# Softmax probabilities moved by sixteen small DMAs a tile, three tiles in four, and one load for the rows of the next branch

## The chip, the cores and the metric

The kernel runs on one core of one Trainium2 chip. The metric is the device time of one launch in microseconds. The profile is that of one execution; its rows give start times from the beginning of its span.

## The reference, cut to what matters

The layer has a token mixer (a gated linear attention, GLA, and a latent attention, MLA, then gates and a projection) and a mixture of 16 experts. The change lies in the latent attention, with 8 heads over 1024 tokens, and in the hand-over to the GLA branch that the kernel computes after it:

```python
def attend(qblk):                       # one block of 128 queries
    s = jnp.einsum('bhqd,bhkd->bhqk', qblk, k_t).astype(jnp.float32) * scale
    p = jax.nn.softmax(s, axis=-1)
    return jnp.einsum('bhqk,bhkd->bhqd', p.astype(v_t.dtype), v_t)
```

All values are float32. Each float32 product is made from three matmuls of high and low parts.

## The kernel before

**Tiles and steps.** The attention is written as a list of steps (i, n): head i (0 to 7), block n of 128 queries (0 to 7), and five steps more, (8, 0) to (8, 4), in which the last head is finished. Tile t = 8i + n is one block of probabilities, 128 queries by 1024 keys. Each of the engines runs its own program in order, and all of them walk over the same list of steps. Semaphores join them: `s_mm` (scores made), `max_ok` (row maximum made), `exp_ok` (exponentials made), `sq_ok` (tile block-transposed), `p_in` (transposed tile landed), `pt_hi` and `pt_lo` (its two parts made), `pv_mm` (half a head multiplied with the values), `ob_ev` (that half scaled into `obS`), `ob_out` (stored), `inv_out` and `inv_in` (inverse row sums stored and spread).

**One step on each engine.**

- TensorE: `scores(t)` (10 matmuls of 512 columns, waits for the exponentials of tile t-2), one `seam` (4 transposes for the next head's queries or keys), `probs_T(t-1)` if the tile before goes by TensorE (8 transposes), `values` (6 or 9 matmuls, at n = 0, 1, 2, 3, 4, 6, 7), `project` for later heads.
- VectorE (DVE): `probs_squares(t-1)` if that tile goes by DMA (one transposition of 32x32 blocks into the single buffer `squares_T`), `row_maximum(t)`, the low part of the seam, `probs_low(t-1)` for a tile from TensorE, `turned_low(t-3)` for a tile from DMA, and work for the next head.
- ScalarE (ACT): the high part of the seam, `probs_high(t-1)` or `turned_high(t-3)`, `exponentials(t)`, `take` of a projection. At (7, 6) and (8, 0) it also splits the first weights and rows of the GLA branch (`dense_hi`, `rows_high`).
- SyncE (SP) issues all DMAs of this stage, in order, and waits in between: `turn_probs(t-1)`, stores of inverse sums and of outputs, loads of the weights of later heads. A wait holds up everything behind it.

**Two ways for a tile.** The product with the values needs the probabilities with keys on partitions. By TensorE, a tile is transposed through PSUM. By DMA, DVE transposes its 32x32 blocks inside each quarter of the partitions, and DMAs carry each block row to its quarter. Before, every second tile (even t, up to 60) goes by DMA: four DMAs to DRAM, wait until they have landed, one DMA back.

**The next branch.** GLA needs the normalised rows again (`carry<-rows_T`, 8 pieces of 512 KB). `load_rows(k)` loads one piece and waits for the piece before it; two pieces are issued at each of the steps (7, 2), (7, 4), (7, 6), (8, 0).

## Time and profile before

| | us |
|---|---|
| time, median of 3 runs | 1960.42 (1959.71 to 1960.89) |
| the profiled execution | 1961.58 |
| its span | 1959.3 |
| TensorE busy in it | 1869.9 (95%) |
| DVE busy | 1373.2 (70%) |
| ACT busy | 1066.3 (54%) |
| mean granted TensorE clock | 0.983 |

The span is what the trace covers. TensorE is busy for all but 89 us of it. Register, semaphore and DMA-issuing instructions aren't counted as busy; DMA issues appear in the time line as SPq.

### The profile page before, as it was taken

Reading aid. Unit: us, or ns where it says so; the run is one execution under the profiler, and the core shown is the slowest. Engines: PE = TensorE matmul, PEld = TensorE weight load, DVE = VectorE, ACT = ScalarE, POOL = GpSimd, SP = SyncE. Lnnn points to the kernel's source line nnn. Section 1 sums busy time; section 2 is a strip of 40 time slices with the busy share of each in tenths; the row PEclk is TensorE's granted clock in tenths of the full one; section 3 lists DMA queues with packets and bytes.
Section 4 is the critical chain, followed back from the end, with each engine's and each line's share of the span. In section 5 each row is a group of like instructions: output and inputs, shape, how many; then the busy total and the mean of one; then the engine's idle time right before and its main releaser. Section 6 shows DMA issues by size and latency. Waiting matters only on the chain.

```text
span 1959.3 us, 26754 instructions
## 1 busy us (share of the span) xinstructions
PE 1869.9 (95%) x9179; PEld 1574.2 (80%) x9179; DVE 1373.2 (70%) x1829; ACT 1066.3 (54%) x1737; POOL 135.3 (7%) x147
## 2 busy tenths in 40 slices
PE   8989999999489999999999999997799999999997
PEld 8978888887368888888888888886688888888886
DVE  5477777777355657565765437835799898998986
ACT  6576666665244334242534222423677777877775
POOL 1021111010000000000000000000000101101010
PEclk9999999999789999999999999998899999999999
DMA  6125454554621111111454544343999999999993
GB/s 207 44 63 129 105 116 107 112 119 108 161 71 44 55 44 47 40 58 29 151 164 137 172 154 161 126 194 118 371 390 401 391 402 400 391 398 390 400 391 78
DMA packets 180666, 364.30 MB, mean 186 GB/s; under 512 B 29377, under 2 KB 99905, under 8 KB 180417
## 3 DMA queue, kind: packets, MB, share of 16 engines
q1 hardware_dynamic: 174784, 346.33, 51.6%
q0 software_dynamic: 4752, 16.78, 3.4%
q8 instruction: 55, 0.90, 0.2%
q14 instruction: 35, 0.28, 0.1%
q10 hardware_dynamic: 1040, 0.00, 0.0%
HBM read 308.37 MB, written 54.69 MB: 185 GB/s over the span
## 4 chain that ended last, share of the span: by engine, by line
PE 84%; DVE 6%; DMA 5%; ACT 2%; issue 1%; SPq 1%; POOL 1%; DVEq 0%; ACTq 0%; POOLq 0%
PE ps L1195 23%; PE ps L1197 23%; PE ps L1196 23%; PE ps L1184 5%; PE ps L1282 3%; PE ps L1491 1%; DMA probs_T<-squares_T 1%; PE ps L1503 1%; DMA carry<-rows_T 1%; PE ps L1321 1%; PE ps L1320 1%; DVE row_max L2042 1%; PE ps L1475 1%; PE ps L1501 1%; SPq L836 1%
## 5 line engine op out<-in xcount | busy, mean ns | idle before, releaser
L1807 DVE TENSOR_TENSOR w_lo<-w_raw,w_hi 128x1024 fp32r<-128x1024 f32 x384 | 442.6, 1218 | 54.8 <-ACT w_hi L3287 54.7
L3287 ACT ACTIVATE w_hi<-w_raw 128x1024 fp32r<-128x1024 f32 x384 | 371.0, 1053 | 0.5 <-PE ps L1197 0.4
L1195 PE MATMUL ps<-w_hi,xeT_hi 128*128 128x512 f32 x512 | 201.2, 393 | 1.0 <-DVE w_lo L1807 0.9
L1197 PE MATMUL ps<-w_hi,xeT_lo 128*128 128x512 f32 x512 | 199.8, 390 | 0.0
L1196 PE MATMUL ps<-w_lo,xeT_hi 128*128 128x512 f32 x512 | 199.2, 389 | 0.0
L1807 DVE TENSOR_TENSOR d_lo<-d_raw,d_hi 128x1024 fp32r<-128x1024 f32 (+1 forms) x66 | 67.2, 1027 | 143.2 <-ACT d_hi L2925 138.5
L1195 PE MATMUL ps<-hT_parts,d_hi 128*128 128x512 f32 x368 | 145.5, 395 | 0.0
L1197 PE MATMUL ps<-hT_parts,d_lo 128*128 128x512 f32 x368 | 144.1, 392 | 0.0
L1196 PE MATMUL ps<-hT_parts,d_hi 128*128 128x512 f32 x368 | 144.1, 392 | 0.0
L1102 POOL TENSOR_TENSOR stat<-stat,minus_half 128x4 f32<-128x4 f32 (+3 forms) x56 | 54.3, 970 | 1165.2 <-DVE stat L1804 1165.1
L2925 ACT ACTIVATE d_hi<-d_raw 128x1024 fp32r<-128x1024 f32 x42 | 44.5, 1060 | 157.1 <-PE ps L1197 87.7
L2042 DVE TENSOR_REDUCE row_max<-ps 128x1 f32<-128x1024 f32 x64 | 77.8, 1215 | 61.2 <-PE ps L1321 61.1
L1195 PEld LDWEIGHTS ps<-w_hi,xeT_hi 128*128 128x128 f32 x512 | 96.1, 188 | 21.3 <-DVE w_lo L1807 1.2
L1195 PE MATMUL ps<-d_hi,hT_parts 128*128 128x512 f32 x288 | 112.6, 391 | 0.0
L1197 PEld LDWEIGHTS ps<-w_hi,xeT_lo 128*128 128x128 f32 x512 | 96.1, 188 | 20.3
L1196 PE MATMUL ps<-d_lo,hT_parts 128*128 128x512 f32 x288 | 112.1, 389 | 0.0
L1197 PE MATMUL ps<-d_hi,hT_parts 128*128 128x512 f32 x288 | 112.1, 389 | 0.0
L1196 PEld LDWEIGHTS ps<-w_lo,xeT_hi 128*128 128x128 f32 x512 | 96.2, 188 | 19.5
L1195 PE MATMUL ps<-w_hi,act_T_hi 128*128 128x512 f32 x256 | 101.3, 396 | 0.8 <-ACT ye L3310 0.8
L1197 PE MATMUL ps<-w_hi,act_T_lo 128*128 128x512 f32 x256 | 99.9, 390 | 0.0
L1196 PE MATMUL ps<-w_lo,act_T_hi 128*128 128x512 f32 x256 | 99.6, 389 | 0.0
L1195 PEld LDWEIGHTS ps<-hT_parts,d_hi 128*128 128x128 f32 x368 | 69.8, 190 | 14.8 <-issue 0.4
(454 smaller groups left out, 4304.8 us busy)
## 6 DMA issues: line engine op xcount, KB each, us to landing
w_raw<-in_w_gate_e SPq DMA_DIRECT2D x128, 512.0 KB, 6.9
w_raw<-in_w_up_e SPq DMA_DIRECT2D x128, 512.0 KB, 7.0
w_raw<-in_w_down_e SPq DMA_DIRECT2D x128, 512.0 KB, 5.8
d_raw<-in_w_in SPq DMA_DIRECT2D x80, 256.0 KB, 3.3
probs_T<-squares_T SPq DMA_DIRECT2D x124, 128.0 KB
pT_lo<-probs_T SPq DMA_DIRECT2D x31, 512.0 KB, 3.4
gates_T<-stage SPq DMA_DIRECT2D x16, 512.0 KB, 2.9
sg<-gates_T SPq DMA_DIRECT2D x16, 512.0 KB, 3.5
```

Of the source, the lines that this page charges most:

```text
L836: sp.dma_start(rows[:, :, q, :], squares_T[q * SQ:(q + 1) * SQ].rearrange("b j c a -> b j (c a)")).then_inc(p_out, 16)
L1102: pool.tensor_tensor(dst, dst, minus_half[:, 0:dst.shape[1]], ALU.pow).then_inc(done, 1)
L1184: ins = pe.transpose(ps[0:rows, bank, j * P:(j + 1) * P], src, ident[:])
L1195: pe.matmul(out_ap, a_hi, b_hi, start=start, stop=False)
L1196: pe.matmul(out_ap, a_hi, b_lo, start=False, stop=False)
L1197: return pe.matmul(out_ap, a_lo, b_hi, start=False, stop=stop)
L1282: mm = pe.matmul(out_ap, src[:, k, toks], w[:, k, :], start=k == 0, stop=k == kc - 1)
L1320: pe.matmul(bank, qr_T[:, q], kr_T[i % 2][:, cols], start=False, stop=False)
L1807: return dve.tensor_tensor(dst, whole, high.bitcast(F32), ALU.subtract)
L2042: dve.tensor_reduce(row_max[:, n:n + 1], ps[:, 2 * (n % 2):2 * (n % 2) + 2, :], mybir.AxisListType.XY, ALU.max, negate=True).then_inc(max_ ...
L2925: nc.scalar.activation(d_hi[:, n % 2, :], d_raw[:, n % 2, :], ACT.Copy).then_inc(d_hi_ok, 1)
L3287: nc.scalar.activation(w_hi[:, n % RING, :], w_raw[:, n % RAW, :], ACT.Copy).then_inc(hi_ok, 1)
```

## The change

Three parts: (1) tiles 0 to 55 with t % 4 != 3 go by DMA (42 tiles instead of 31), none of the last head; each goes from `squares_T` straight to its place in SBUF by 16 DMAs of 32 partitions x 1 KB, without DRAM. The next block transposition waits until all 16 have landed. (2) The rows for GLA come in one DMA of 4 MB at step (7, 2). (3) `values` at n = 1 stands ahead of the scores of its step.

```diff
 def by_dma(t):
-    return 0 <= t < 8 * MH - 2 and t % 2 == 0
+    return 0 <= t < 8 * (MH - 1) and t % 4 != 3
...
             def turn_probs(t):
-                d, group = t // 2, t // Q4
-                sp.wait_ge(sq_ok, d + 1)
-                rows = p_dram[d % SLOTS].rearrange("(j b) q x -> b j q x", b=SQ)
-                for q in range(Q4):
-                    sp.dma_start(rows[:, :, q, :],
-                                 squares_T[q * SQ:(q + 1) * SQ].rearrange("b j c a -> b j (c a)")).then_inc(p_out, 16)
-                sp.wait_ge(p_out, 16 * Q4 * (d + 1))
-                if d:
-                    sp.wait_ge(p_in, 16 * d)
+                group = t // Q4
+                sp.wait_ge(sq_ok, dma_count(t))
                 if group >= 2:
                     sp.wait_ge(pv_mm, group - 1)
-                sp.dma_start(probs_part(pT_lo, t).bitcast(F32),
-                             p_dram[d % SLOTS].rearrange("p q (c a) -> p q c a", a=SQ)).then_inc(p_in, 16)
+                low = probs_part(pT_lo, t).bitcast(F32)
+                for q in range(Q4):
+                    for j in range(Q4):
+                        sp.dma_start(low[j * SQ:(j + 1) * SQ, q],
+                                     squares_T[q * SQ:(q + 1) * SQ, j]).then_inc(p_in, 16)
...
+                if m == 2 * MH - 1:
+                    sp.wait_ge(p_in, 16 * Q4 * Q4 * dma_count(NT * MH - 1))
...
+                    if i == MH - 1:
+                        sp.wait_ge(h_out, 32)
+                        sp.wait_ge(seam_tr, MH * 8)
+                        sp.dma_start(hT_again, h_dram.rearrange("k p s -> p k s")).then_inc(hT_in, 16)
...
-                if n % 2 == 0 and 8 * (MH - 1) + 2 <= 8 * i + n:
-                    for k in range(2):
-                        if 8 * i + n - 8 * (MH - 1) - 2 + k < KD:
-                            load_rows(8 * i + n - 8 * (MH - 1) - 2 + k)
...
             for i, n in STEPS:
+                if pv_at(i, n) and n == 1:
+                    values(*pv_at(i, n))
                 if i < MH:
                     scores(i, n)
...
-                if pv_at(i, n):
+                if pv_at(i, n) and n != 1:
                     values(*pv_at(i, n))
...
             def probs_squares(t):
                 dve.wait_ge(exp_ok, t + 1)
                 if t:
-                    dve.wait_ge(p_out, 16 * Q4 * (t // 2))
+                    dve.wait_ge(p_in, 16 * Q4 * Q4 * (dma_count(t) - 1))
```

DVE's order in head 2 shows the tiles that follow each other closely. Before, from the transposition of tile 20 to that of tile 22 (`row_max` is the row maximum of a step, `pT_lo<-pT_lo` is `turned_low`, `pT_lo<-ps` is `probs_low`):

```order
L2057 STREAM_TRANSPOSE squares_T<-probs 128x1024 [waits p_out,exp_ok]
L2042 TENSOR_REDUCE row_max<-ps 128x1 [waits s_mm]
L1807 TENSOR_TENSOR kr_lo<-ps,kr_T 128x512 [waits seam_hi]
L1807 TENSOR_TENSOR pT_lo<-pT_lo,pT_hi 128x1024 [waits pt_hi]
L2042 TENSOR_REDUCE row_max<-ps 128x1 [waits s_mm]
L2031 SCALAR_TENSOR_TENSOR qT_lo<-ps,qhn_c,qT_hi 128x512 [waits seam_hi]
L1807 TENSOR_TENSOR pT_lo<-ps,pT_hi 128x4x4x32 [waits pt_hi] x2
L1991 TENSOR_TENSOR qR<-qR,stat 128x4x192 [waits rstd]
L2057 STREAM_TRANSPOSE squares_T<-probs 128x1024 [waits p_out,exp_ok]
```

The same stretch of DVE's program now, tiles 20, 21 and 22:

```order
L2050 STREAM_TRANSPOSE squares_T<-probs 128x1024 [waits p_in,exp_ok]
L2035 TENSOR_REDUCE row_max<-ps 128x1 [waits s_mm]
L1800 TENSOR_TENSOR kr_lo<-ps,kr_T 128x512 [waits seam_hi]
L1800 TENSOR_TENSOR pT_lo<-pT_lo,pT_hi 128x1024 [waits pt_hi]
L2050 STREAM_TRANSPOSE squares_T<-probs 128x1024 [waits p_in,exp_ok]
L2035 TENSOR_REDUCE row_max<-ps 128x1 [waits s_mm]
L2024 SCALAR_TENSOR_TENSOR qT_lo<-ps,qhn_c,qT_hi 128x512 [waits seam_hi]
L1984 TENSOR_TENSOR qR<-qR,stat 128x4x192 [waits rstd]
L2050 STREAM_TRANSPOSE squares_T<-probs 128x1024 [waits p_in,exp_ok]
```

A third transposition stands between the two, one step after the first, and each waits for `p_in` of the one before; the row maximum of the step is behind it.

SP's order in the last head, before (from the store of head 6's first half, step (7, 2)):

```order
L829 DMA mla_out_T<-obS 128x512 [waits ob_ev]
L859 DMA obS<-inverse_sums 128x512 [waits ob_out,inv_out]
L867 DMA carry<-rows_T 128x1024 [waits seam_tr,h_out]
L867 DMA carry<-rows_T 128x1024 [waits hT_in]
L836 DMA probs_T<-squares_T 32x4x256 [waits sq_ok]
L836 DMA probs_T<-squares_T 32x4x256 x3
L843 DMA pT_lo<-probs_T 128x1024 [waits pv_mm,p_in,p_out]
L851 DMA inverse_sums<-row_inv 128x4x1 [waits inv_in,inv_ok]
L829 DMA mla_out_T<-obS 128x512 [waits ob_ev]
L867 DMA carry<-rows_T 128x1024 [waits hT_in] x2
```

and now, from the same store up to the first weights of GLA (`d_raw`) at step (7, 6):

```order
L830 DMA mla_out_T<-obS 128x512 [waits ob_ev]
L858 DMA obS<-inverse_sums 128x512 [waits ob_out,inv_out]
L879 DMA carry<-rows_T 128x8x1024 [waits seam_tr,h_out]
L848 DMA inverse_sums<-row_inv 128x4x1 [waits inv_in,inv_ok]
L830 DMA mla_out_T<-obS 128x512 [waits ob_ev]
L858 DMA obS<-inverse_sums 128x512 [waits ob_out,inv_out]
L778 DMA d_raw<-in_w_in 128x4x128 x4
```

The waits for each piece of the rows and for the tiles of the last head are gone from SP's queue.

## Rows read from the trace of the kernel before

**Rows 1.** The page's busy time: engine, us, share, instructions.
```profile
PE 1869.9 (95%) x9179; PEld 1574.2 (80%) x9179; DVE 1373.2 (70%) x1829; ACT 1066.3 (54%) x1737; POOL 135.3 (7%) x147
```

**Rows 2.** Windows of head 2 and of the end of attention.
```profile
core 0: us, PE busy (x) PEld busy (x) DVE busy (x) ACT busy (x) POOL busy (x), PEclk, DMA share, GB/s
...
224.10:275.60 51.50, 51.13 (x289) 43.96 (x289) 39.34 (x60) 31.98 (x79) 5.53 (x5) 1.00 0.51 114
...
481.00:568.20 87.20, 52.90 (x226) 42.69 (x225) 37.87 (x42) 29.79 (x41) 3.19 (x6) 0.84 0.55 130
```

**Rows 3.** SP's turn issues to DRAM of tile 0, tile 8, tile 56, and its last.
```profile
131.35 1.81 SPq L836 DMA_DIRECT2D probs_T<-squares_T  x4
...
172.58 2.38 SPq L836 DMA_DIRECT2D probs_T<-squares_T  x4
...
481.06 1.77 SPq L836 DMA_DIRECT2D probs_T<-squares_T  x4
...
520.34 1.89 SPq L836 DMA_DIRECT2D probs_T<-squares_T  x4
```

**Rows 4.** Block transpositions (31), minimum, median, maximum ns, first and last start.
```profile
L2057 DVE STREAM_TRANSPOSE squares_T<-probs x31: 1211/1239/1247, 130.1 to 507.0; 128x1024 f32<-128x1024 f32 x31
```

**Rows 5.** SP's time line in head 2: start, us, line, transfer, count.
```profile
234.59 0.43 SPq L829 DMA_DIRECT2D mla_out_T<-obS  x1
238.70 0.32 SPq L859 DMA_DIRECT2D obS<-inverse_sums  x1
```

**Rows 6.** SP's time line at 683 us, small DMAs in a row.
```profile
683.47 1.27 SPq L805 DMA_DIRECT2D w_a<-in_gla_wa_f  x3
684.83 1.29 SPq L805 DMA_DIRECT2D w_a<-in_gla_wa_b  x3
686.22 0.37 SPq L807 DMA_DIRECT2D b_a<-in_gla_ba_f  x1
```

**Rows 7.** Time from issue to landing of line 805's DMAs (8 KB each).
```profile
DMA to landing us min/median/max: 1.5/2.0/3.0
```

**Rows 8.** Windows between the transpositions of tiles 18 and 20, and 22 and 24.
```profile
236.73:253.08 16.35, 16.35 (x93) 14.38 (x92) 11.92 (x24) 9.71 (x26) 2.01 (x2) 1.00 0.46 142
262.74:274.33 11.59, 11.41 (x66) 9.60 (x65) 9.31 (x19) 7.55 (x19) 0.00 (x0) 1.00 0.48 158
```

**Rows 9.** TensorE's time line in the last head and after, idle time before in brackets.
```profile
484.30 1.03 PE L1184 MATMUL ps<-ident,probs 128*128 128x128 f32 x8
485.09 0.48 PE L1195 MATMUL ps<-pT_hi,v_hi_even 128*128 128x512 f32 x1
...
498.30 1.82 PE L1184 MATMUL ps<-ident,probs 128*128 128x128 f32 x8 [4.10 <-ACT probs L2916]
...
538.59 1.97 PE L1184 MATMUL ps<-ident,probs 128*128 128x128 f32 x8 [17.44 <-ACT probs L2916]
...
568.19 1.19 PE L1403 MATMUL ps<-gateT,w_a_split 80*128 80x512 f32 x2 [7.04 <-DVE w_a_split L1807]
```

**Rows 10.** SP's time line in the last head.
```profile
526.29 2.08 SPq L777 DMA_DIRECT2D d_raw<-in_w_in  x4
528.41 7.58 SPq L867 DMA_DIRECT2D carry<-rows_T  x2
```

**Rows 11.** ACT's time line in the last head.
```profile
532.65 1.06 ACT L2925 ACTIVATE d_hi<-d_raw 128x1024 fp32r<-128x1024 f32 x1 [16.25 <-DMA d_raw<-in_w_in]
```

**Rows 12.** The page's DMA issues: count, KB each, median us to landing.
```profile
d_raw<-in_w_in SPq DMA_DIRECT2D x80, 256.0 KB, 3.3
...
carry<-rows_T SPq DMA_DIRECT2D x12, 512.0 KB, 4.4
```

**Rows 13.** The page's bytes moved, GB/s in 40 slices.
```profile
GB/s 207 44 63 129 105 116 107 112 119 108 161 71 44 55 44 47 40 58 29 151 164 137 172 154 161 126 194 118 371 390 401 391 402 400 391 398 390 400 391 78
```

**Rows 14.** DVE's outputs of head 6's first and head 7's second half.
```profile
484.16 0.69 DVE L2078 TENSOR_TENSOR obS<-ps,obS 128x512 f32<-128x512 f32 x1
...
561.40 0.69 DVE L2078 TENSOR_TENSOR obS<-ps,squares_T 128x512 f32<-128x512 f32 x1 [11.03 <-DMA mla_out_T<-obS]
```

More of the change, by code:

```diff
@@ L64 @@
 Q4 = P // SQ
-SLOTS = 4
 LATE = NT - 2
@@ L168, in tensor_count, with dma_count @@
     return sum(by_tensor(u) for u in range(t + 1))
+def dma_count(t):
+    return sum(by_dma(u) for u in range(t + 1))
 def parts_count(t):
@@ L236, in hybrid_layer @@
     h_dram = nc.dram_tensor("rows_T", (KD, P, S), F32, kind="Internal").ap()
-    p_dram = nc.dram_tensor("probs_T", (SLOTS, P, Q4, NT * SQ), F32, kind="Internal").ap()
     inv_dram = nc.dram_tensor("inverse_sums", (2, HALF), F32, kind="Internal").ap()
@@ L541, in hybrid_layer @@
         sq_ok = sem("sq_ok")
-        p_out = sem("p_out")
         p_in = sem("p_in")
@@ L639, in hybrid_layer @@
         s_sig = Later(latT_act, 7)
-        g_out = [Later(h_out, 32), Later(hT_in, 16 * KD)]
+        g_out = [Later(h_out, 32), Later(hT_in, 16)]
         rows_out = Later(inv_out, 32 * MH)
@@ L858, in spread_inverse @@
                     sp.wait_ge(ob_out, 16 * m)
+                if m == 2 * MH - 1:
+                    sp.wait_ge(p_in, 16 * Q4 * Q4 * dma_count(NT * MH - 1))
                 sp.dma_start(inverse_at(h, half), spread(inv_dram[half], HALF)).then_inc(inv_in, 16)
-            def load_rows(k):
-                if k == 0:
-                    sp.wait_ge(h_out, 32)
-                    sp.wait_ge(seam_tr, MH * 8)
-                else:
-                    sp.wait_ge(hT_in, 16 * k)
-                sp.dma_start(hT_again[:, k, :], h_dram[k]).then_inc(hT_in, 16)
             load_ukv(2)
@@ L2903, in turned_high @@
             def turned_high(t):
-                act.wait_ge(p_in, 16 * (t // 2) + 16)
+                act.wait_ge(p_in, 16 * Q4 * Q4 * dma_count(t))
                 nc.scalar.activation(probs_part(pT_hi, t), probs_part(pT_lo, t).bitcast(F32), ACT.Copy).then_inc(pt_hi, 1)
@@ L2910, in exponentials @@
                 if by_dma(t - 2):
-                    act.wait_ge(sq_ok, (t - 2) // 2 + 1)
+                    act.wait_ge(sq_ok, dma_count(t - 2))
                 elif t >= 2:
@@ L2957, in rows_high @@
             def rows_high(k):
-                act.wait_ge(hT_in, 16 * (k + 1))
+                act.wait_ge(hT_in, 16)
                 nc.scalar.activation(hT_hi[:, k, :], hT_again[:, k, :], ACT.Copy,
```

## The prediction, as it was made

> **What bounds the kernel now.** I read the page's busy times first: TensorE is busy for 95% of the span [rows 1]. Then I cut the attention into windows of one head each, since a mean over 1959 us says nothing about this stage [rows 2]. The reader is to see that head 2 (heads 1 and 3 to 5 read alike) takes 51.5 us with TensorE busy for 51.1 of them and DVE for 39.3: TensorE sets the pace there, about 6.4 us a step. From SP's turn of tile 0 at 131.35 to that of tile 8 at 172.58, head 0 takes 41.2 us; from tile 0 to tile 56, at 481.06, the seven heads take 349.7 us [rows 3]. The last window is another matter: 87.2 us with only 52.9 us of TensorE, and its granted clock is 0.84 where the others have 1.00 [rows 2]. The time line of that window shows gaps in front of TensorE, of 4.10, 17.44 and 7.04 us, and one more between the first two [rows 9]. So two stretches are to be judged: seven heads in which TensorE must not be starved, and an end in which it is.
>
> **One tile by sixteen DMAs.** In the changed order each transposition of a DMA tile waits for `p_in` of the DMA tile before, and the row maximum of the step stands behind that transposition in DVE's queue. Tiles 0, 1, 2 of every four stand in steps that follow each other, so one cycle is: transpose, issue 16, land, transpose again.
>
> - The transposition: 1.24 us [rows 4].
> - Issues: SP's smallest DMAs in a row, 16 rows of 512 bytes, start 0.46 us apart: from 683.47 to 686.22 there are six intervals, 2.75/6 = 0.458 [rows 6]. The present turns, each DMA four times larger than a new one, take 1.77 us for four, 0.44 each, when nothing holds them up [rows 3]. Size makes no difference in these rows, so I take 0.46 for a DMA of 32 KB: the sixteenth starts 15 x 0.46 = 6.9 us after the first.
> - Landing: 1.5/2.0/3.0 us for DMAs of 8 KB from DRAM into SBUF [rows 7]. The trace has no transfer from SBUF to SBUF, so this is the nearest row; I take 1.7, between its least and its median, since the new ones leave DRAM out, and keep 1.5 and 2.7 for the bounds.
> - Sum of a cycle: 1.24 + 6.9 + 1.7 = 9.8, with about 0.1 for two hand-overs by semaphore 9.9 us, against steps of 6.4.
>
> TensorE can't hide it: `scores(t)` wait for the exponentials of t-2, these for the row maximum, and that is behind the transposition. ACT is held up in the same way.
>
> **A head, interval by interval.** Tiles 0 to 1, 1 to 2, 4 to 5, 5 to 6 are direct cycles: 4 x 9.9 = 39.6. From 2 to 4 there are two steps, and DVE's own work counts: between the transpositions of tiles 18 and 20 it is busy for 11.92 us [rows 8]; one more `turned_low` (1.2) and waits of some 0.4 make 13.5. In step (i, 2) SP stores `obS`, and the load after it comes 4.1 us later [rows 5]; SP is then about 2.0 us late for tile 2, a cycle of 11.9, which the 13.5 cover. From 6 to the next head's 0 DVE has 9.31 [rows 8] + 1.2 = 10.5. Together 63.6 us for heads 1 to 5. Head 0 has five cycles and one of 10.4, since no head before it is finished there: 59.9. Head 6 has no next but one to prepare: 4 x 9.9 + 11.9 + 10 = 61.5. Sum: 59.9 + 5 x 63.6 + 61.5 = 439.4, against 349.7: **+90 us**.
> What TensorE saves in these heads (28 tiles by transposes before, 14 after, 0.79 us each, 484.30 to 485.09 in [rows 9]; 11 us) is worth nothing while it waits for the chain. Nor does a lower clock after each gap cost, as steps of 9.9 us have room for 6.4 us of work partly at half speed. SP alone would fit: 48 x 0.46 = 22 us for every four steps and some 2 besides, in 25.8; it is the single buffer that puts transposition, issue and landing in a row.
>
> **`values` at n = 1 ahead of the scores.** Six matmuls move ahead of ten in TensorE's queue, so a half of the head is ready about 2.3 us earlier, `turn_probs` of the next group no longer waits for `pv_mm`, and the scores come 1.4 us later. All of it lies inside steps that the chain holds up: 0. If the chain didn't, it would lie beside a busy TensorE, and be 0 again.
>
> **The end of attention.** The three tiles of head 7 that went by DMA now cost 3 x 0.79 = 2.4 us of TensorE and take away the turns that SP stood in. The first two gaps go: both waited for exponentials [rows 9], which stood in ACT's queue behind a turned tile. So does part of the third: ACT waited 16.25 us for `d_raw` [rows 11], whose load SP issued only at 526.29, between pieces of the rows of which each waits for the one before [rows 10].
> When does it go on now? I keep the clock of before for the start of head 7. The last seam is long done; the 4 MB follow the store of the half that DVE finished at 484.85 [rows 14] by the 4.1 us of [rows 5] and an issue: 489.5. At 390 GB/s, as in the experts [rows 13], they take 10.7 us, and 1.5 to start: 501.7. The stores of step (7, 4) go through the same queue, so they land at about 502.5; then SP spreads the inverse sums and issues the first weights, done at 504; they land 3.3 us later [rows 12]. ACT splits weights and a row (2 x 1.06 [rows 11]), takes tile 62's high parts and the last exponentials (1.1 + 1.3): 513 with the hand-overs. So the transposes that started at 538.59 [rows 9] start at 513: **25 us** earlier. TensorE's own work would be done at about 506, so a gap of some 7 us stays.
> The fourth gap: DVE waited 11.03 us for the first half's store [rows 14], which SP issued behind the last two pieces, and then had the low parts of four rows to make ahead of the gate weights. Now the rows are there and SP is free; TensorE's 22.6 us of work between its last two gaps (568.19 - 7.04 - 538.59) leave time for all but 1.5 us. 5.5 us of gap go, and about 1.5 us by a clock that falls less far (eight transposes took 1.97 us behind the long gap, 1.03 without one [rows 9]): **7 us**. The end together: **-32 us**.
>
> **Sum.** +90 - 32 = +58 us on the profiled execution's 1961.58 (span 1959.3, the rest lies around it): 2019.6. It stands 1.2 us above the median of the runs: 2018.
>
> **Two rules against each other.** The trace puts 0.46 us on each issue [rows 6]. The Trainium skill, DMA: Bandwidth & Descriptors, section SWDGE vs HWDGE vs iDMA, says that the sequencer's time to start a DMA is usually small beside the DMA itself; by that the cycle would be little more than transposition and landing, and the time that of the first rival. The same page's Rules for kernel authors says to coalesce, since transfers under 64 KB pay mostly overhead. The trace is with the second: its small DMAs cost SP as much as large ones.
>
> **The rivals.**
>
> - *The chain fits behind TensorE (faster).* The place is the transposition's wait for `p_in`, the price the cycle. Were sixteen issues overlapped, so that a cycle takes under 6.4 us, nothing would be lost in the heads, 11 us of transposes saved and 32 us gained at the end: 1961.6 - 43 = 1919, 1917 by the median. On the way there the loss falls by 30 us for each us of cycle (30 of the 42 intervals are bound by it), so gain and loss meet at 8.0 us, that is at 0.33 us an issue with the same landing. For it: an issue by itself takes 0.32 us [rows 5]. Against it: in a row they come 0.44 to 0.46 apart for every size in the trace.
> - *Issues stall as they do now (slower still).* SP's turn issues of before, from the group at 131.35 to the one at 520.34, 31 groups of four [rows 3], sum up to 68.3 us, 0.55 each. With that mean the cycle is 11.2 us and more intervals are bound by it: 30 x 1.3 + 5 x 0.7 = 42 us more, 2060. With a landing of 2.7 on top it would be near 2100.
> - *The end gives little back.* The 4 MB stand ahead of the stores and of the first weights in the same queue. If they run at the 4.4 us of a 512 KB piece by itself [rows 12], 35 us in all, ACT waits to about 536 and the end gives 9 us: 2041.
> - *Gain and loss cancel*, at a cycle of about 8.0 us: 1960.
>
> **Chances.** The forecast, with a cycle between 9.1 us (0.42 an issue, landing 1.5: 24 us less) and 10.7 (25 us more): 0.60, its own range 1994 to 2043. Stalls 0.13, little back 0.13, chain fits or nearly 0.12, cancel 0.02. To hold 8 in 10 I go down to a cycle of 8.4 us (0.37 an issue, the shortest of [rows 6] with the pause behind it taken as nothing, and 1.5) and up past the stalls: 1972 to 2066. A measurement of this kernel tells changes over about 0.2%, 4 us, from none. Faster by more: 0.12; within: 0.02; slower: 0.86.
>
> **What would show it.** In the profile after: transpositions of tiles 0, 1, 2 of a group start 9.9 us apart, each after several us of DVE idle until a DMA landed; SP's sixteen issues of a tile take 7.3 us; heads 1 to 5 take about 63 us with TensorE busy for 50 or so of them; the chain that ended last has SP's issues and DMAs in it through the seven heads. In the last head one gap of about 7 us stands ahead of the last tile's transposes. It is wrong if sixteen issues take under 5.5 us, if DVE doesn't wait for `p_in`, or if the gap at the weights stays near 17 us.

## The result, and the profile after

The changed kernel takes 2180.6 us (2179.0 to 2183.9), the kernel before 1960.3 beside it: a ratio of 1.113, 95% interval 1.111 to 1.1145. Slower was right; +58 us was forecast and it is +220, far outside the range of 1972 to 2066 us.

The page of the changed kernel: busy times, the clock that TensorE was granted in 40 slices, and the chain that ended last, by engine and by line.

```profile
PE 1918.5 (88%) x9091; PEld 1609.6 (74%) x9091; DVE 1384.3 (64%) x1829; ACT 1069.3 (49%) x1726; POOL 135.8 (6%) x147
...
PEclk9988888987987899999999999999979999999999
...
PE 70%; SPq 14%; DVE 7%; DMA 4%; ACT 2%; issue 2%; POOL 1%; DVEq 0%; ACTq 0%; POOLq 0%
PE ps L1186 20%; PE ps L1188 20%; PE ps L1187 20%; SPq L840 13%; PE ps L1175 3%; DMA pT_lo<-squares_T 3%; DVE squares_T L2050 2%; PE ps L1273 2%; PE ps L1484 1%; PE ps L1496 1%; DMA mla_out_T<-obS 1%; DVE row_max L2035 1%; PE ps L1468 1%; P
```

SyncE's issues of line 840, the sixteen small DMAs, are 13% of the chain. TensorE has fewer instructions than before [rows 1] and is busy for 49 us more: it is stretched by its clock, not by work. Head 1, from the transposition of tile 8 to that of tile 16, as a window (columns as in [rows 2]: length, busy time of PE, PE's loads, DVE, ACT and POOL, granted clock, DMA share, GB/s):

```profile
208.90:294.60 85.70, 57.51 (x274) 48.79 (x273) 41.27 (x62) 32.45 (x77) 5.55 (x4) 0.84 0.23 56
```

85.7 us where head 1, like the head 2 of [rows 2], took 51.5, at a granted clock of 0.84 where it was 1.00. Heads 1 to 5 take 82.2 to 87.7 us (forecast about 63), with TensorE busy for 56 to 58 of them. The group of `squares_T`, with its duration in ns (least, median, most), its waits, and the time to landing:

```profile
L840 SPq DMA_DIRECT2D pT_lo<-squares_T x672: 507/591/5441, 131.3 to 713.4; - x168
L2050 DVE STREAM_TRANSPOSE squares_T<-probs x42: 1233/1245/1247, 130.0 to 702.7; 128x1024 f32<-128x1024 f32 x42
...
  DMA pT_lo<-squares_T: 241.7, 29
...
DMA to landing us min/median/max: 1.8/1.8/8.1
```

So DVE stood 241.7 us, 29 times, in front of a transposition. [Rows 4] showed 31 transpositions in 377 us; now there are 42 in 573. SyncE's and DVE's time lines from the last tile of head 0 on and in head 1:

```profile
195.96 10.01 SPq L840 DMA_DIRECT2D pT_lo<-squares_T  x16
208.79 0.37 SPq L848 DMA_DIRECT2D inverse_sums<-row_inv  x1
210.51 25.60 SPq L840 DMA_DIRECT2D pT_lo<-squares_T  x32
236.15 0.58 SPq L830 DMA_DIRECT2D mla_out_T<-obS  x1
```

```profile
224.83 1.25 DVE L2050 STREAM_TRANSPOSE squares_T<-probs 128x1024 f32<-128x1024 f32 x1 [7.00 <-DMA pT_lo<-squares_T]
237.44 1.25 DVE L2050 STREAM_TRANSPOSE squares_T<-probs 128x1024 f32<-128x1024 f32 x1 [8.93 <-DMA pT_lo<-squares_T]
```

Sixteen issues take 10.0 us (forecast 7.3), 0.633 us from start to start, and two transpositions in a row start 12.6 us apart: 1.24 + 15 x 0.633 + 1.8, and 0.1 for the hand-overs. The end of attention (the answer to [rows 9 to 11]), on TensorE's, ACT's and SyncE's time lines:

```profile
762.03 1.97 PE L1175 MATMUL ps<-ident,probs 128*128 128x128 f32 x8 [14.48 <-ACT probs L2909]
...
786.62 0.78 PE L1396 MATMUL ps<-gateT,w_a_split 80*128 80x512 f32 x2 [1.91 <-DVE w_a_split L1800]
```

```profile
756.09 1.06 ACT L2918 ACTIVATE d_hi<-d_raw 128x1024 fp32r<-128x1024 f32 x1 [12.78 <-DMA d_raw<-in_w_in]
```

```profile
728.54 0.38 SPq L879 DMA_DIRECT2D carry<-rows_T  x1
735.47 0.37 SPq L848 DMA_DIRECT2D inverse_sums<-row_inv  x1
736.05 0.34 SPq L830 DMA_DIRECT2D mla_out_T<-obS  x1
749.93 0.33 SPq L858 DMA_DIRECT2D obS<-inverse_sums  x1
750.32 2.08 SPq L778 DMA_DIRECT2D d_raw<-in_w_in  x4
```

The gap at the gate weights is 1.9 us where it was 7.0, but the one ahead of the last tile is still 14.5: ACT waits for weights that SyncE can't issue until the stores of the inverse sums and of the output's half, issued at 735.47 and 736.05, have landed, 14 us later. I had the 4 MB of line 879 in mind for that wait. The experiments will put it elsewhere.

### The profile page after: what moved, and what is told of

The parts are those of the page before. It is cut to its first block, busy times and chain, and to the rows that moved or that the text cites. A ratio compares the mean times of both kernels' runs of the same rounds, so it can differ in the third digit from the quotient of the medians.

```text
span 2177.1 us, 27084 instructions
## 1 busy us (share of the span) xinstructions
PE 1918.5 (88%) x9091; PEld 1609.6 (74%) x9091; DVE 1384.3 (64%) x1829; ACT 1069.3 (49%) x1726; POOL 135.8 (6%) x147
## 4 chain that ended last, share of the span: by engine, by line
PE 70%; SPq 14%; DVE 7%; DMA 4%; ACT 2%; issue 2%; POOL 1%; DVEq 0%; ACTq 0%; POOLq 0%
PE ps L1186 20%; PE ps L1188 20%; PE ps L1187 20%; SPq L840 13%; PE ps L1175 3%; DMA pT_lo<-squares_T 3%; DVE squares_T L2050 2%; PE ps L1273 2%; PE ps L1484 1%; PE ps L1496 1%; DMA mla_out_T<-obS 1%; DVE row_max L2035 1%; PE ps L1468 1%; PE ps L1494 1%; DVE affT L2668 1%
## 5 line engine op out<-in xcount | busy, mean ns | idle before, releaser
L2050 DVE STREAM_TRANSPOSE squares_T<-probs 128x1024 f32<-128x1024 f32 x42 | 52.2, 1243 | 242.0 <-DMA pT_lo<-squares_T 241.7
L2909 ACT ACTIVATE probs<-ps,row_max 128x1024 f32<-128x1024 f32 x64 | 71.5, 1117 | 192.2 <-DVE row_max L2035 192.2
L1273 PE MATMUL ps<-w_uq_h,cqT 128*128 128x192 f32 x384 | 84.1, 379 | 64.8 <-DVE d_hi L2024 28.8
L1273 PEld LDWEIGHTS ps<-w_uq_h,cqT 128*128 128x128 f32 x384 | 75.9, 224 | 72.6 <-DVE d_hi L2024 31.5
L1186 PE MATMUL ps<-w_kv_hi,ckvT_hi 128*128 128x256 f32 x96 | 36.3, 378 | 97.7 <-DVE qT_lo L2024 67.5
```

The costliest lines, as they stand in the source:

```text
L1186: pe.matmul(out_ap, a_hi, b_hi, start=start, stop=False)
L1273: mm = pe.matmul(out_ap, src[:, k, toks], w[:, k, :], start=k == 0, stop=k == kc - 1)
L2050: dve.transpose(squares_T[:], probs[:, t % 2, :].rearrange("p (c j b) -> p j c b", c=NT, j=Q4)) \
L2909: nc.scalar.activation(probs[:, t % 2, :].rearrange("p (a c) -> p a c", a=2), ps[:, 2 * (n % 2):2 * (n % 2) + 2, :], ACT.Exp, bias=row_max ...
```

## Experiments

Medians, each beside runs of the kernel before on the same chip (1960.3 to 1965.5 us there); ratios are to those. e2, e8, e9 and e13 leave out a part of the computation, which the text of each names; m1 to m3 are small kernels with one execution each.

```
kernel                                             us      ratio (95% interval)
changed kernel                                     2180.6  1.113  (1.111 - 1.1145)
e1  every second tile within SBUF                  1993.9  1.0165 (1.0148 - 1.0182)
e2  four DMAs a tile                               2005.7  1.0221 (1.0204 - 1.0238)
e3  two halves, two semaphores                     2117.4  1.0789 (1.0771 - 1.0807)
e4  two queues                                     2095.0  1.0680 (1.0662 - 1.0698)
e5  before + rows in one load, values, last head   1953.2  0.9942 (0.9929 - 0.9956)
e6  e5 with the rows in two loads                  1951.8  0.9936 (0.9922 - 0.9949)
e7  before + values moved                          1973.2  1.0045 (1.0031 - 1.0059)
e8  changed kernel, sums in 128 pieces             2154.8  1.0986 (1.0967 - 1.1004)
e9  e2, sums in 128 pieces                         1958.2  0.9982 (0.9972 - 0.9991)
e10 e6, sums block-transposed before the store     1936.4  0.9868 (0.9851 - 0.9884)
e11 e10, values moved in the last head alone       1927.5  0.9834 (0.9820 - 0.9847)
e12 before, sums block-transposed                  1937.2  0.9882 (0.9866 - 0.9897)
e13 e4, sums in 128 pieces                         2056.5  1.0485 (1.0469 - 1.0501)
```

My theory after the result: the chain that I had described, with an issue of 0.63 us in place of 0.46. Its rivals: that copies within SBUF get in each other's way or in the engines', that the clock is the cause and not the consequence, that something else holds the transposition.

### What one issue costs

m1, issues alone. Two of its ten series as code:

```
for q in range(Q4):                                       # within SBUF, series 1
    for j in range(Q4):
        sp.dma_start(low[j*SQ:(j+1)*SQ, q, 0:256], sq[q*SQ:(q+1)*SQ, j]).then_inc(done, 16)
for q in range(Q4):                                       # to DRAM, series 2
    for j in range(Q4):
        sp.dma_start(dr_b[q, j*SQ:(j+1)*SQ, 0:256], sq[q*SQ:(q+1)*SQ, j]).then_inc(done, 16)
```

> A kernel that leaves the layer out: SyncE alone issues series of 16 DMAs, each series ended by a wait for all of them and run four times, in this order: (1) the changed kernel's 16 copies within SBUF, 32 partitions x 1 KB each; (2) the same from SBUF to DRAM; (3) the same from DRAM to SBUF; (4) within SBUF, 128 partitions x 1 KB; (5) within SBUF, 16 partitions x 1 KB; (6) within SBUF, 32 x 4 KB; (7) SBUF to DRAM in the form of the kernel before, 32 x 4 x 1 KB; (8) within SBUF, 1 partition x 1 KB; (9) four DMAs of 32 x 4 KB within SBUF; (10) one DMA of 128 x 4 KB. Theory (an issue costs by its kind: both sides in SBUF 0.63 us, one in DRAM 0.46): series 1, 4, 5, 6 and 8 all near 0.63, series 2, 3 and 7 near 0.46. Rival (the cost goes by the number of descriptors): 1 partition and 16 partitions cheaper than 32, 128 partitions dearer. Rival (the cost comes from the queue filling up with DMAs that are not yet done): the first issues of a series at 0.46 and the later ones slower, and 128 x 1 KB slower than 32 x 1 KB. Landing after the last issue 1.5 to 2 us in each.

The groups of its lines 270 to 303, series 1 to 8 in the order of that text (duration of the issue in ns, least, median, most; first and last start):

```profile
L270 SPq DMA_DIRECT2D low<-sq x64: 507/591/592, 47.0 to 90.5; - x64
...
L275 SPq DMA_DIRECT2D dr_b<-sq x64: 302/421/423, 92.4 to 124.5; - x64
...
L280 SPq DMA_DIRECT2D low<-dr_a x64: 302/421/438, 126.1 to 159.2; - x64
...
L284 SPq DMA_DIRECT2D low<-sq x64: 465/601/603, 161.1 to 205.4; - x64
...
L289 SPq DMA_DIRECT2D low<-sq x64: 507/589/591, 207.5 to 250.8; - x64
...
L294 SPq DMA_DIRECT2D low<-sq x64: 507/591/598, 252.5 to 297.2; - x64
...
L298 SPq DMA_DIRECT2D dr_b<-sq x64: 302/446/466, 299.5 to 340.4; - x64
...
L303 SPq DMA_DIRECT2D low<-sq x64: 497/589/591, 344.5 to 387.1; - x64
```

Read the medians against the names on the left: every group from SBUF to SBUF has 0.59 to 0.60 us, whether 1, 16, 32 or 128 partitions and whether 1 KB or 128 KB; every group with one side in DRAM has 0.42 to 0.45. The distance from start to start is 0.04 more, 0.63 and 0.46 (0.64 for 128 partitions in series 4, 0.49 for the 128 KB of series 7). The least duration in a group (0.507 and 0.302) is that of an issue after a wait, not in a row. Landing after the last issue was 1.8 us in series 1. The price hangs on where the two sides lie, and on nothing else that I varied by more than 0.03 us. A second such kernel (m2, series 5 and 6) added that a copy within the same partitions and one from DRAM to DRAM also cost 0.59: both sides in the same kind of memory. Theory confirmed; the rivals of piece count and of a filling queue fell.

### How many issues, through what

e2, four issues a tile:

```diff
                 for q in range(Q4):
-                    for j in range(Q4):
-                        sp.dma_start(low[j * SQ:(j + 1) * SQ, q],
-                                     squares_T[q * SQ:(q + 1) * SQ, j]).then_inc(p_in, 16)
+                    j = (q + 1) % Q4
+                    sp.dma_start(low[j * SQ:(j + 1) * SQ], squares_T[q * SQ:(q + 1) * SQ]).then_inc(p_in, 16)
```

> The changed kernel with 4 DMAs a tile in place of 16: each takes a quarter of the transposed tile (32 partitions x 4 KB) to the next quarter's partitions, so that the same 512 KB move within SBUF for the same 42 tiles, but the blocks are not sorted to their places (that part of the computation is left out). Theory (the number of issues is what costs): cycle 1.24 + 4 x 0.63 + 1.8 = 5.6 us, under a step of 6.4, the wait at the transposition goes, heads near 52 us, 1935 to 1965 us. Rival (bytes within SBUF or their landing cost): the wait stays, over 2100 us.

With the same bytes in a quarter of the issues 175 of the 220 us go: it is their number that costs, not bytes within SBUF. (The pieces are also fewer and larger here, 4 KB in place of 1 KB; that an issue's price doesn't go by them is m1's result.) Transpositions in a row start 5.5 us apart, as expected (5.6). But 2005.7 is above my 1965: DVE still waited 74.8 us. One wait shows where, on SyncE's and on DVE's time line:

```profile
210.22 0.37 SPq L847 DMA_DIRECT2D inverse_sums<-row_inv  x1
212.41 0.34 SPq L830 DMA_DIRECT2D mla_out_T<-obS  x1
213.56 10.48 SPq L840 DMA_DIRECT2D pT_lo<-squares_T  x5
```

```profile
222.26 1.25 DVE L2049 STREAM_TRANSPOSE squares_T<-probs 128x1024 f32<-128x1024 f32 x1 [5.89 <-DMA pT_lo<-squares_T]
```

Four issues from 213.56 are out by 216.0 (the fifth of the row belongs to the next tile), yet the transposition that waits for them starts at 222.26: over 6 us to land in place of 2.7, its median here. In the transfers' records of this run eleven stretches up to 520 us show packets of 1 to 3 us each (4 KB take 0.3 otherwise), and each begins 4 to 7 us after a store of inverse sums. In the kernel before, 15 such stretches of 4 to 8 us follow 15 stores by 3 to 7 us. That store, `inverse_sums<-row_inv`, writes 512 pieces of 4 bytes. e8 and e9 below test it.

e1, fewer tiles:

```diff
 def by_dma(t):
-    return 0 <= t < 8 * (MH - 1) and t % 4 != 3
+    return 0 <= t < 8 * (MH - 1) and t % 2 == 0
```

> The changed kernel with every second tile of heads 0 to 6 turned within SBUF (28 tiles, 16 DMAs each) in place of three of four; the last head by TensorE, rows of the next branch in one load, as in the changed kernel. Theory (16 issues at 0.63 us in a chain with the transposition and the landing, 12.6 us a tile): the chain fits under two steps of the kernel before (2 x 6.4 = 12.9 us), so the transposition's wait on the DMAs all but goes; heads near 53 us, and the time is that of before less what the end gives (10 to 15 us) plus a few microseconds where an issue stalls: 1950 to 1975 us. Rival (copies from SBUF to SBUF slow the engines or the other transfers, whatever the chain): 28/42 of the growth stays, 2100 us or more, without waits at the transposition. Rival (the growth is in TensorE's clock): heads over 56 us, 2000 us.

1993.9: most of the growth goes, but I had expected 1950 to 1975, and DVE still waited 55.0 us, 17 times, for the copies. "Two steps are 12.9 us" was a mean again. In the kernel before the intervals between the transpositions of a head are 9.3, 12, 13.9 and 16.3 us; the chain lifts the first two to 12.6, and the long ones, full of TensorE's work, don't shrink for it. That is 4 us a head; heads 3 and 4 take 62 us each (53 to 57 the others), and copies are held up there as in e2: sixteen issues from 325.65 on, 3.6 us behind a store of inverse sums, take 15.5 us in place of 10.0. The rival of 28/42 of the growth (2100) fell. The rival of the clock had named 2000 us, close to this; but head 1, 55 us long, had a granted clock of 1.00, so that it grew without it. In heads 3 and 4, at 0.94 and 0.95, TensorE was busy for 1.4 and 3.2 us longer than before, of 10 to 11 us that they grew by.

e3, without the single buffer's chain:

```diff
-                dve.transpose(squares_T[:], probs[:, t % 2, :].rearrange("p (c j b) -> p j c b", c=NT, j=Q4)) \
-                    .then_inc(sq_ok, 1)
+                for j in range(2):
+                    if t:
+                        dve.wait_ge(p_in[j], 32 * Q4 * (dma_count(t) - 1))
+                    dve.transpose(squares_T[:, 2 * j:2 * j + 2],
+                                  probs[:, t % 2, :].rearrange("p (c j b) -> p j c b", c=NT, j=Q4)[:, 2 * j:2 * j + 2]) \
+                        .then_inc(sq_ok, 1)
```

> The changed kernel with the tile transposed in two halves, each with its own semaphore: the first half of the next tile is transposed once the first 8 DMAs of this one have landed, while the last 8 are issued. The 16 DMAs a tile stay. Theory (the wait is a chain of issue, landing and transposition through one buffer; without the last two SyncE's issue alone bounds it): a tile costs 16 x 0.633 = 10.1 us in place of 12.6, with SyncE's other work and its stalls 64 to 70 us a head in place of 82: 2065 to 2100 us. Rival (what holds the transposition is not the buffer but, for instance, the time at which the exponentials are ready): no change, 2170 to 2190 us.

2117.4, above my 2065 to 2100. The heads fell from 85 to 76.5 us, so that the chain through the one buffer was part of it, against the rival; sixteen issues (10.0 us a tile) remain. My 64 to 70 a head left out the stretches after the stores, which this trace has too (a transposition at 324.12 waits 9.0 us for copies issued behind the store at 311.02). What they cost here no run separates; in the changed kernel it is 3 us a head (e8), so that they needn't be all of what I missed.

e4, the issues shared; SyncE keeps `q` 0 and 1, and ScalarE has this ahead of the exponentials:

```diff
+            def turn_probs(t):
...
+                act.wait_ge(sq_ok, dma_count(t))
...
+                for q in range(2, Q4):
+                    for j in range(Q4):
+                        nc.scalar.dma_start(low[j * SQ:(j + 1) * SQ, q],
+                                            squares_T[q * SQ:(q + 1) * SQ, j]).then_inc(p_in, 16)
...
+                if i < MH and by_dma(8 * i + n - 1):
+                    turn_probs(8 * i + n - 1)
                 if i < MH:
                     exponentials(i, n)
```

> The changed kernel with 8 of a tile's 16 DMAs issued by ScalarE's queue (ahead of the exponentials of the next tile) and 8 by SyncE's. Theory (serial issue on one engine): 1.24 + 8 x 0.63 + 1.8 = 8.1 us a tile, per four tiles 2 x 8.1 and 12.9 = 29 us, heads 58 us, if ScalarE's issues cost it no more than SyncE's: 2010 to 2040 us; ScalarE, which waited 192 us for DVE, takes 8 x 0.63 us a tile in that time. Rival (the DMA engines or SBUF serve these copies one after the other, and the issue only shows it): the pitch of each queue doubles to 1.2 us, and the time stays at 2180 us or grows.

2095.0 where I had expected 2010 to 2040, heads of 73 us. ScalarE's time line:

```profile
245.15 5.31 ACTq L2908 DMA_DIRECT2D pT_lo<-squares_T  x8
250.56 1.11 ACT L2920 ACTIVATE probs<-ps,row_max 128x1024 f32<-128x1024 f32 x1 [5.58 <-issue]
```

Eight issues take 5.3 us there while SyncE issues its eight, so the pitch doesn't double and the DMA engines aren't what is served in turn. But ScalarE computes nothing meanwhile: the exponentials come 5.6 us later. I had given it that time, and it is on the path (DVE waited 59.1 us for exponentials, and still 81.3 us for copies). The Trainium skill, DMA: Bandwidth & Descriptors, section Issuing engines are not separate DMA queues, says that issuing on several engines only saves the sequencer's time, "usually small relative to the DMA itself". The first half agrees with this run. The second doesn't: 0.6 us for each DMA against 1.8 us to landing, and eight of them hold the engine 5.3 us.

### The end of attention

e7, one part alone:

```diff
             for i, n in STEPS:
+                if pv_at(i, n) and n == 1:
+                    values(*pv_at(i, n))
                 if i < MH:
                     scores(i, n)
```

> The kernel before with the product with the values ahead of the scores at the second step of each head, and nothing else. I forecast 0 for this. Theory: the same time within 0.2% (1956 to 1964 us). Rival: the row maximum of the second tile comes later by the product's length in each head and TensorE waits for the exponentials, 8 x 1 to 3 us slower, 1968 to 1985 us.

1973.2, 0.45% or 9 us slower than before in place of 0. Up to 480 us TensorE's waits at line 1282 (queries' projection, for DVE's `qr_T`) are 9.6 us in six times, and 1.1 us before: 1.4 us in each head. The later scores delay the row maximum, and behind it DVE's low part of the query. My "beside a busy TensorE" overlooked that TensorE next reads what DVE makes behind that maximum. What it costs in the changed kernel, where the chain holds those steps, no run shows.

e5, the change's end without its heads (with the change's edits to the rows and to `values` in the kernel before), and e6, e5 with the rows in two loads:

```diff
-    return 0 <= t < 8 * MH - 2 and t % 2 == 0
+    return 0 <= t < 8 * (MH - 1) and t % 2 == 0
```

```diff
-                        sp.dma_start(hT_again, h_dram.rearrange("k p s -> p k s")).then_inc(hT_in, 16)
+                        sp.dma_start(hT_again[:, 0:2], h_dram[0:2].rearrange("k p s -> p k s")).then_inc(hT_in, 16)
...
                     load_gla(0, 1)
+                    sp.dma_start(hT_again[:, 2:], h_dram[2:].rearrange("k p s -> p k s")).then_inc(hT_in, 16)
```

> The kernel before, with its turning through DRAM, and only the parts of the change at the end: the last head all by TensorE, the product with the values ahead of the scores at the second step, the rows of the next branch in one load of 4 MB. My forecast of this part was -32 us; the changed kernel's trace shows -10 us up to the last tile's transposition and -15 us up to the gate logits. Theory (the part is worth what the trace shows): 1945 to 1950 us. Rival (the gain was made only because the changed kernel's heads left room ahead of it): 1960 us or more.

> As the run before it, but the 4 MB of rows in two loads: the first two blocks (1 MB) where the one load stood, the other six (3 MB) behind the loads of the next branch's weights. Theory (the small store of the inverse sums and the weights wait behind the 4 MB in the DMA queues, which holds the exponentials' engine 12.8 us before the last tile): the wait of 12.8 us goes to a few, another 8 to 12 us gained, 1935 to 1942 us. Rival (the weights are not late for the rows' sake, or the rows are then late themselves at the step that reads the third block): no more than 2 us either way.

e5 has 1953.2, between my 1945 to 1950 and the rival's 1960: 0.58% under its runs of before, 11 us, with e7's loss in it. The end's other parts are worth some 20 us, so the gain isn't lent by the changed kernel's heads. e6 has 1951.8 where I had expected 1935 to 1942, no difference from e5 that can be told. TensorE's last gap in e6, and SyncE ahead of it:

```profile
534.89 1.97 PE L1177 MATMUL ps<-ident,probs 128*128 128x128 f32 x8 [11.85 <-ACT probs L2911]
```

```profile
502.19 1.01 SPq L880 DMA_DIRECT2D carry<-rows_T  x1
510.97 0.37 SPq L851 DMA_DIRECT2D inverse_sums<-row_inv  x1
511.55 0.34 SPq L829 DMA_DIRECT2D mla_out_T<-obS  x1
522.89 0.33 SPq L859 DMA_DIRECT2D obS<-inverse_sums  x1
```

Only 1 MB of rows is ahead now and the spreading load still goes out 12 us after the store of the sums. My theory for e6, that the 4 MB hold it, fell: the gap was 13.35 us in e5, so that 3 MB less ahead took 1.5 us off it. The store's own 512 pieces were left.

### The store of the inverse sums

e8 and e9, in the changed kernel and in e2:

```diff
-                sp.dma_start(inv_dram[half].rearrange("(t p) -> p t", p=P), row_inv[:, Q4 * half:Q4 * half + Q4],
-                             allow_slow_non_contiguous=True).then_inc(inv_out, 16)
+                sp.dma_start(inv_dram[half].rearrange("(p t) -> p t", p=P),
+                             row_inv[:, Q4 * half:Q4 * half + Q4]).then_inc(inv_out, 16)
```

> The changed kernel with the inverse sums stored in 128 pieces of 16 bytes in place of 512 of 4 bytes (so they are not put in the order of the rows: that part of the computation is left out). Theory (each of these stores is followed by a stretch of about 6 us in which copies take 2 to 3 us each; where it falls on a tile's 16 copies the chain waits): two stores a head, some hit an idle moment of the queue; the changed kernel's trace shows two landings or issues held by 5 us and some smaller: 10 to 50 us less than 2180, 2130 to 2170 us. Rival (the stretches don't come from this store): 2175 to 2185 us. The chain of 12.6 us a tile stays in both, so the time stays over 2100 us.

> The kernel with four DMAs a tile (blocks not sorted) and the inverse sums in 128 pieces of 16 bytes (not in the order of the rows). With four DMAs the time was 2005.7 us, heads of 60 us, and the one long wait a head (6 to 8 us) lay on copies issued 3 to 5 us after the store of inverse sums. Theory: that wait goes, heads 53 to 54 us, 1950 to 1970 us. Rival (the long wait has another cause): 2000 to 2010 us.

2154.8 and 1958.2, both as the theory had it: 26 and 48 us for one store's form. The stretches of slow packets are gone: by the count that gives the 15 in the kernel before (five or more packets of up to 4 KB and over 1 us each, close together), neither trace has one. In head 2 of e8 the transpositions stand 13.3, 12.6, 16.9, 12.9, 12.7 and 13.7 us apart, and the end reads:

```profile
738.18 1.97 PE L1175 MATMUL ps<-ident,probs 128*128 128x128 f32 x8 [6.03 <-ACT probs L2909]
```

```profile
720.07 0.32 SPq L848 DMA_DIRECT2D inverse_sums<-row_inv  x1
720.65 0.32 SPq L830 DMA_DIRECT2D mla_out_T<-obS  x1
726.09 0.32 SPq L858 DMA_DIRECT2D obS<-inverse_sums  x1
```

The 4 MB load is still one piece, and the gap is 6.0 us in place of 14.5; I had forecast 7. The last spreading load waits for the store of sums alone: it follows that by 1.4 us (741.62 to 743.03), and by 8.2 us in the changed kernel (765.47 to 773.62). So the forecast of the end was missed by what it didn't look at.

e12, with the whole computation kept and in the kernel before; e10 and e11 put it beside e6's end:

```diff
-                dve.reciprocal(row_inv[:, at], row_sum[:, at]).then_inc(inv_ok, 1)
+                dve.reciprocal(row_inv[:, 0:Q4], row_sum[:, at]).then_inc(inv_ok, 1)
+                dve.wait_ge(inv_ok, 2 * m + 2)
+                dve.transpose(inv_T[:], row_inv[:]).then_inc(inv_ok, 1)
...
+                for q in range(Q4):
+                    sp.dma_start(inv_dram[half].rearrange("(t q b) -> q t b", q=Q4, b=SQ)[q],
+                                 inv_T[q * SQ:q * SQ + Q4]).then_inc(inv_out, 16)
```

> The kernel before, with nothing changed but the store of inverse sums: block-transposed in SBUF and stored by 4 DMAs of 4 pieces of 128 bytes (all of the computation kept). Theory (the stretches of slow packets after the stores cost the kernel before as well): with it the 12 us of waits at the transposition and some of the end go, 1944 to 1952 us; together with the end's parts it gave 15 us. Rival (it paid only beside the changed end): 1956 to 1962 us.

> The kernel with turning through DRAM, the end as in the changed kernel and the rows in two loads (1951.8 us), and the inverse sums block-transposed in SBUF ahead of their store, which then is 4 DMAs of 4 pieces of 128 bytes in place of one of 512 pieces of 4 bytes (all of the computation is kept). Theory (the stretches of slow packets that follow the stores go): in the kernel before they lie mostly under TensorE's work; the waits that they make are 12 us in all, half of it on the path: 1940 to 1950 us, a few us less than the run without. Rival (all of it is hidden, and the 3 issues and two small operations more cost): 1951 to 1956 us.

> The kernel with turning through DRAM, the rows in two loads and the inverse sums block-transposed before their store (1936.4 us), with the product with the values ahead of the scores in the last head alone, where the all-TensorE turning needs it, in place of every head. Theory (in the heads before it the move makes TensorE wait 1.6 us a head for DVE's low part of the query's rotary rows, which gave 9 us alone): 7 to 10 us less, 1926 to 1931 us. Rival (with the other changes that wait is hidden): 1934 to 1938 us.

e12 takes 1937.2, 23 us less than before and more than I had expected (8 to 16); e10 takes 1936.4, also below my 1940. In e12 the first six heads are as long as before (tile 48 is transposed at 429.3 us, 429.9 before), though DVE's waits for copies at the transposition, 12.3 us before, go down to 0.9; some 3 us are made in head 6 (tile 56 at 476.5, 479.8 before) and the rest at the end. TensorE's gaps there, 14.9 us in all, to hold against 34.3 before, the 4.10, 17.44 and 7.04 of [rows 9] and this one:

```profile
512.70 1.97 PE L1184 MATMUL ps<-ident,probs 128*128 128x128 f32 x8 [5.71 <-ACT probs L2916]
```

```profile
501.41 1.97 PE L1186 MATMUL ps<-ident,probs 128*128 128x128 f32 x8 [2.78 <-ACT probs L2923]
...
520.32 1.97 PE L1186 MATMUL ps<-ident,probs 128*128 128x128 f32 x8 [10.20 <-ACT probs L2923]
...
545.14 0.70 PE L1405 MATMUL ps<-gateT,w_a_split 80*128 80x512 f32 x2 [1.91 <-DVE w_a_split L1809]
```

e11, with `values` moved in the last head alone (tile 56's high parts would otherwise overwrite what the last product of head 6's first half reads), takes 1927.5:

```diff
-                if pv_at(i, n) and n == 1:
+                if pv_at(i, n) and (i, n) == (MH - 1, 1):
                     values(*pv_at(i, n))
```

That is 9 us less than e10, as e7 said, and 1.7% less than before. Against e12 it is 10 us less: with the short store the other parts of the end are worth half of their 20 us in e5. Its gap ahead of the last tile:

```profile
513.50 1.97 PE L1179 MATMUL ps<-ident,probs 128*128 128x128 f32 x8 [3.58 <-ACT probs L2918]
```

e13, e4 with e8's edit:

> The kernel with a tile's 16 DMAs issued 8 by SyncE and 8 by ScalarE (2095.0 us), and the inverse sums in 128 pieces of 16 bytes (not in the order of the rows). Theory (what it has over the 2010 to 2040 us that I worked out is in part the slow stretches after the stores, in part ScalarE's issues, which hold the exponentials): 25 to 50 us of it go, 2045 to 2070 us. Rival (it is ScalarE's issues alone): 2085 to 2097 us.

2056.5, heads of 68 us, 38 us under e4: the stores have their part in e4's excess, as the theory had it. DVE's wait of 59.1 us for ScalarE stays, which fits ScalarE's issues as the other part; no run takes them out alone.

m2 and m3, the store by itself, first with a wait behind it, then without:

```
sp.dma_start(inv_d[0:512].rearrange("(t p) -> p t", p=P), sq[:, 0, 0:4], allow_slow_non_contiguous=True)
sp.dma_start(inv_d[512:1024].rearrange("(p t) -> p t", p=P), sq[:, 0, 0:4])
```

> A kernel that leaves the layer out: SyncE alone issues, four times each, (1) 32 copies within SBUF of 32 partitions x 1 KB; (2) the store of inverse sums as the kernels have it (512 elements of 4 bytes, each a piece of its own, to DRAM), a wait for it, and the 32 copies; (3) the same with the store in 128 pieces of 16 bytes; (4) the spreading load of the sums from DRAM to 128 partitions, a wait, and the 32 copies; (5) 16 copies of 32 x 1 KB whose source and target are the same partitions; (6) 16 copies of 32 x 1 KB from DRAM to DRAM. Theory (in the layer, packets of other transfers take 2 to 3 us each in a stretch of about 6 us that begins 3 to 5 us after each store of inverse sums, because of its 512 pieces): series 2 alone shows packets over 1 us or a landing or an issue of 3 us and more; in 3 there are none or shorter ones. Rival (the stretch comes from something else in the layer, such as instruction fetches of the busy engines): none in any series. The issue: 0.63 us in 1, 5 and 6 (both sides in the same memory) by the first series of measurements; a rival that only crossing between partitions costs has 5 at 0.46.

> A kernel that leaves the layer out: SyncE issues, four times each, (1) three sets of 16 copies within SBUF (32 partitions x 1 KB), a wait after each set; (2) the store of 512 pieces of 4 bytes and, with no wait for it, the same three sets; (3) the store of 128 pieces of 16 bytes and the same. In the measurement before, a wait for the first store took 8 to 9 us and for the other 1.1 us, and copies after the wait ran as ever. Theory (the store holds the DMA engines for those 8 us): in series 2 the first set of 16 is done 3 to 8 us late or an issue in it takes 3 us and more, in 3 nothing does. Rival (the store's pieces wait in the memory alone and copies pass them): the sets of series 2 take as long as those of series 1, and the layer's slow stretches need the layer's other traffic.

SyncE's time line in m2: the store of 512 pieces (line 278), then that of 128 (line 283), each with the copies that wait for it:

```profile
132.64 0.40 SPq L278 DMA_DIRECT2D inv_d<-sq  x1
140.98 20.14 SPq L272 DMA_DIRECT2D low<-sq  x32
...
253.47 0.34 SPq L283 DMA_DIRECT2D inv_d<-sq  x1
254.89 20.13 SPq L272 DMA_DIRECT2D low<-sq  x32
```

8.3 us against 1.4 for 2 KB either way; landings of 8.0 to 9.3 us in all four. The copies behind the wait run as ever (20.1 us for 32). In m3 the copies don't wait, and of four sets of 48 behind the large store one took 34.7 us and one 33.3, the others 32.5 and 32.6 like those without it. So I expected too much of m3: by itself the store is slow to complete but lets copies pass with 0 to 2 us of delay. Why copies in the layer are held for 5 us is open; that they are, and no longer are with the store's other form, e9 shows. The Trainium skill, DMA: Bandwidth & Descriptors, section Rules for kernel authors, says that a last dimension that isn't contiguous becomes a descriptor for each element and should be rearranged. This trace agrees: the window of one store has 528 packets in the first form and 144 in the second, and the rearranged one lands after 1.4 us in place of 8.3.

## Why the prediction was wrong

- **The mechanism stood.** The single buffer puts transposition, issue and landing in a row; DVE waits for `p_in`, the row maximum and the exponentials stand behind it. The transposition (1.24) and the landing (1.7 forecast, 1.8) were right.
- **The term that failed is the issue**, "0.46 for a DMA of 32 KB". It is 0.633 when both sides are in SBUF. My rows were from DRAM to SBUF and from SBUF to DRAM [rows 3, 6]; they showed that size makes no difference, and I concluded that kind doesn't either. The cycle is 12.6 in place of 9.9. 28 direct intervals at 2.7 us are 76 us. In e8 those 28 take 13.0 us in the mean, so +87; the 11 us more lie in intervals where SyncE has other DMAs to issue between.
- **The two-step intervals**, 13.5 and 10.5 us by DVE's own work, were measured at 16.7 and 13.7 (e8, means over heads 1 to 5): +43 in the seven heads. Two steps failed. TensorE's window in [rows 8] was 16.35 us and full, and I summed DVE's 11.92. And "Nor does a lower clock after each gap cost" is wrong there (in e8's interval from tile 10 to tile 12, 17.0 us, TensorE is busy for 14.0 at a granted clock of 0.80 and waits 3.0): the projection of line 1273, 2.2 us for twelve matmuls at full clock, takes 3.6 and 3.8 us behind the waits at 227.9 and 240.5, at a granted clock of 0.84 over the head. How much of the 43 us is the clock's and how much the full window's is not shown.
- **The stretches after the stores** weren't in the sum: 14 us in the heads and 10 us at the end (changed kernel against e8).
- **The end**, -32 forecast: with the stores' stretches gone it lacks 6 us up to the last tile (49.4 us from tile 54's transposition, forecast 43.4) and no more behind it. The step that failed is "they land at about 502.5", 0.8 us behind the 4 MB: the stores took 14 us, and 5.4 with the sums in 128 pieces (e8). The rival "the end gives little back" blamed the 4 MB; e6 says that this was the wrong suspect, though the 9 us that it gave the end back are near the changed kernel's 10 up to the last tile.
- **`values`, 0:** wrong in its second half ("0 again" if the chain didn't hold): 9 us (e7). For the changed kernel itself no run tests the 0 alone.
- Together 87 + 43 + 14 + 10 + 6 = 160 of the 162 us that were missed. These are differences between the forecast and the traces, stretch by stretch, so that they must come near the whole; the causes of the 87, 14 and 10 have experiments behind them, those of the 43 and the 6 only the traces.
- **The rival of stalls** was priced at 0.55 an issue from [rows 3]. The true cost was above even that, so no case of mine held it. No row showed the operation at all; a price for it that is multiplied by 15 and then by 42 asked for a bound of its own above the rows, and the range had only the stalls' 0.55.

## What to carry to other kernels

Price an issue by its kind (which memories the two sides are in) before multiplying it by hundreds; where the trace has none of that kind, let the range say so. Lay a periodic chain against each interval of the schedule, not against their mean: the short ones pay and the long ones give nothing back. And when an engine waits for a transfer at the end of a stage, look at the smallest store in the queue before the largest load: sixteen stores of 2 KB in 512 pieces each were worth 1.2% of this kernel.

## What the hardware showed that I had not expected

- An issue by SyncE costs 0.63 to 0.64 us from start to start when both sides are in SBUF, for 1 KB as for 128 KB, and as much when both are in DRAM (32 KB); when they differ it costs 0.46 (32 KB) to 0.49 (128 KB).
- A store of 512 pieces of 4 bytes completes in 8.0 to 9.3 us; 128 pieces of 16 bytes take 1.4 us.
- Eight issues on ScalarE's queue kept that engine from computing for 5.3 us.
- TensorE's granted clock fell to 0.82 to 0.86 over heads 1 to 5, each with four waits of TensorE of 3 to 14 us, and its busy time of 51.1 us [rows 2] grew by 9 to 13% in them.
